# Diagonal tap weights, gate halves and decay products moved in a one-core block kernel

## The reference, cut to what matters

```
proj = h @ w_in[i]
p_r, p_k, p_v, p_c, z_rwkv, z_conv = split(proj)
# rwkv7: k, r times cumulated decays, triangular inverse per chunk of the keys, state recurrence
y_rwkv = rwkv7_time_mix(h, p_r, p_k, p_v, ...)
# convolution
u, gate = split(p_c)
c = u * sigmoid(gate)
c = causal_depthwise_conv(c, dw, 31 taps) + dw_b
y_conv = silu(layer_norm(c)) @ w_conv_out
merged = sigmoid(z_rwkv) * y_rwkv + sigmoid(z_conv) * y_conv
```

## Time and profile before

| what | value |
| --- | --- |
| median of 3 runs (lowest, highest) | 1400.84 us (1398.81, 1406.21) |
| the profiled execution | 1398.78 us, its span 1396.7 us |
| PE busy | 1332.3 us, 95% of the span |
| DVE busy | 1003.6 us, 72% |
| ACT busy | 772.5 us, 55% |
| POOL busy | 105.7 us, 8% |
| mean granted TensorE clock | 0.981 |

### The profile page before, as it was taken

One profiled execution on the slowest core, in us unless ns is written; L12 is line 12 of the kernel. 1 busy time (PEld: TensorE's weight loads), 2 busy tenths in 40 slices (PEclk: granted clock), 3 DMA queues, 4 the chain that ended last, 5 costly groups with the idle time before them and its releaser, 6 DMA issues.

```text
span 1396.7 us, 30214 instructions
## 1 busy us (share of the span) xinstructions
PE 1332.3 (95%) x12462; PEld 1266.0 (91%) x12462; DVE 1003.6 (72%) x1655; ACT 772.5 (55%) x1348; POOL 105.7 (8%) x133
## 2 busy tenths in 40 slices
PE   5999989999999999999997899999999998999998
PEld 5998948989989999989995799999999887999986
DVE  4769897978876664475899867886565655888754
ACT  4596496549455443454668655444455455644453
POOL 2000100000001110000101001111000100022100
PEclk8999999999999999999999899999999999999999
DMA  7642620213545546546662264556565521555462
GB/s 224 186 147 94 211 92 3 93 63 111 191 152 161 185 137 209 187 129 204 195 207 83 75 197 154 185 175 197 174 202 173 163 86 43 200 182 184 155 214 69
DMA packets 199859, 212.71 MB, mean 152 GB/s; under 512 B 8972, under 2 KB 191020, under 8 KB 199612
## 3 DMA queue, kind: packets, MB, share of 16 engines
q1 hardware_dynamic: 197180, 201.46, 45.2%
q0 software_dynamic: 2464, 9.52, 2.3%
q10 hardware_dynamic: 96, 0.02, 0.0%
HBM read 209.33 MB, written 1.65 MB: 151 GB/s over the span
## 4 chain that ended last, share of the span: by engine, by line
PE 83%; DVE 8%; ACT 4%; SPq 2%; issue 1%; DMA 1%; DVEq 0%; ACTq 0%
PE pb L450 21%; PE pb L452 21%; PE pb L451 21%; DVE w_lo L496 1%; PE pb L2678 1%; PE pb L2679 1%; PE pb L2677 1%; PE pb L2198 1%; ACT pj L961 1%; PE pb L2187 1%; SPq L602 1%; DVE pj L1626 1%; PE pb L2604 1%; DMA raw<-in_ffn_w_down_dram 1%; PE pb L2302 1%
## 5 line engine op out<-in xcount | busy, mean ns | idle before, releaser
L490 ACT ACTIVATE w_hi<-raw 128x1024 fp32r<-128x1024 f32 (+2 forms) x384 | 396.7, 1041 | 317.4 <-PE pb L452 248.4
L496 DVE TENSOR_TENSOR w_lo<-raw,w_hi 128x1024 fp32r<-128x1024 f32 (+2 forms) x384 | 467.6, 1221 | 136.9 <-ACT w_hi L490 136.0
L450 PE MATMUL pb<-x_hi,w_hi 128*128 128x256 f32 x1920 | 549.6, 286 | 6.0 <-DVE x_lo L1387 3.8
L451 PE MATMUL pb<-x_lo,w_hi 128*128 128x256 f32 x1920 | 546.5, 285 | 0.0
L452 PE MATMUL pb<-x_hi,w_lo 128*128 128x256 f32 x1920 | 546.4, 285 | 0.0
L450 PEld LDWEIGHTS pb<-x_hi,w_hi 128*128 128x128 f32 x1920 | 371.7, 194 | 9.2 <-DVE w_lo L496 6.6
L451 PEld LDWEIGHTS pb<-x_lo,w_hi 128*128 128x128 f32 x1920 | 371.7, 194 | 0.2
L452 PEld LDWEIGHTS pb<-x_hi,w_lo 128*128 128x128 f32 x1920 | 371.5, 193 | 0.0
L742 POOL TENSOR_TENSOR sub<-sub,rstd 128x256 f32<-128x256 f32 x66 | 71.9, 1104 | 593.0 <-ACT sub L1113 593.0
L450 PE MATMUL pb<-act_hi,w_hi 128*128 128x256 f32 x392 | 112.1, 286 | 3.5 <-DVE w_lo L496 3.5
L452 PE MATMUL pb<-act_hi,w_lo 128*128 128x256 f32 x392 | 111.8, 285 | 0.0
(11 more groups left out here) (344 smaller groups left out, 2197.7 us busy)
## 6 DMA issues: line engine op xcount, KB each, us to landing
raw<-in_ffn_w_up_dram SPq DMA_DIRECT2D x55, 1024.0 KB, 5.1
raw<-in_w_in_dram SPq DMA_DIRECT2D x28, 1024.0 KB, 5.1
raw<-in_ssd_w_in_dram SPq DMA_DIRECT2D x20, 1024.0 KB, 5.4
raw<-in_ffn_w_down_dram SPq DMA_DIRECT2D x16, 1024.0 KB, 5.1
raw<-in_fox_w_in_dram SPq DMA_DIRECT2D x16, 1024.0 KB, 5.8
raw<-in_ffn_w_down_dram SPq DMA_DIRECT2D x16, 896.0 KB, 5.2
raw<-in_ffn_w_gate_dram SPq DMA_DIRECT2D x11, 1024.0 KB, 5.3
raw<-in_ssd_w_out_dram SPq DMA_DIRECT2D x8, 1024.0 KB, 5.2
```

What stands on the lines that cost most here:

```text
L450: pe.matmul(o, w_hi[m][:, k, :], hi[:, k0 + k, :], start=first and k == 0, stop=False)
L451: pe.matmul(o, w_hi[m][:, k, :], lo[:, k0 + k, :], start=False, stop=False)
L490: act.activation(piece(ly, u, w_hi[m], nk, m), raw_piece(ly, u, s, nk, m), ACT.Copy).then_inc(sem("w_hi_ready"), 1)
L496: dve.tensor_tensor(piece(ly, u, w_lo[m], nk, m), raw_piece(ly, u, s, nk, m), piece(ly, u, w_hi[m], nk, m).bitcast(F32), ALU.subtract).the ...
```

## The change

- The ring of diagonal blocks gets 56 places in place of 24: 32 in the slot ZC and 24 in the last six tiles of the slot ZR. ScalarE writes the first 56 blocks (28 taps) inside `ug`, three taps behind each block from block 4, in place of the first 24 behind the sigmoid. At block 4 it first waits for `PAIRS_MADE`, at block 9 for `R_DECAYED`. `DIAG_LEAD` is 22 in place of 8.
- The gate's sigmoid and the product u times gate are made in two halves of four tiles: the first on ScalarE at block 13 and on VectorE at block 14, the second behind `ug`. TensorE waits for the first alone (`GLU_MADE` stays 4; `INVERSES_MADE` becomes 6). ScalarE no longer waits for `GLU_MADE` before its next weights.
- The mixes of v come behind blocks 0 to 3, and the two decay products behind blocks 5 and 6, after the triangular eviction. `lab_t` moves to other tiles of `sub`, since TMP is still read by then.
- The two memsets of `mt` move to GpSimd, between the two hops of its transfers. VectorE waits for them before the first substitution step that reads.
- `SUB_STEPS` holds one step more, so that 15 steps lie in `ug`; the first of the larger corner steps takes the place of the last small one behind `ug`.
- The third `z` eviction, not the ninth, waits for the end of the convolution, as ZR now holds blocks.

The diff, cut to its core:

```diff
-        PE_TILES, NDIAG, DIAG_LEAD = 2 * PE_PAIRS, 24, 8
-        diag = [slot(ZC)[:, i // 4, HEAD * (i % 4):HEAD * (i % 4) + HEAD] for i in range(NDIAG)]
+        PE_TILES, NDIAG, DIAG_LEAD = 2 * PE_PAIRS, 56, 22
+        diag_tiles = [slot(ZC)[:, i, :] for i in range(KC)] + [slot(ZR)[:, i, :] for i in range(2, KC)]
+        diag = [t[:, HEAD * i:HEAD * i + HEAD] for t in diag_tiles for i in range(4)]
+        DIAG_BLOCK, DIAG_STEPS = 4, 3
-        LAB_BLOCK, SUB_BLOCK, SUB_STEPS = 2, 8, (3, 3, 2, 2, 1, 1, 1, 1)
+        LAB_BLOCK, SUB_BLOCK, SUB_STEPS = 2, 8, (3, 3, 3, 2, 1, 1, 1, 1)
-        lab_t = region[:, 0:RWKV_HEADS * T // 4]
+        lab_t = flat_sub[:, 2048:2048 + RWKV_HEADS * T // 4]
...
             pool.wait_ge(sem("mixed"), 3 * KC)
+            link(pool.memset(mt, 0.0))
+            link(pool.memset(mt.rearrange("p s t -> p (s t)")[:, 0:CHUNK * CHUNK:CHUNK + 1], 1.0))
+            pool.nop().then_inc(sem("pool_stages"), 1)
...
+            def gate_half(h):
+                act.wait_ge(sem("evac_done"), L["ug"].evac0 + BANKS + KC + 4 * h + 4)
+                t = slot(GATE)[:, 4 * h:4 * h + 4, :]
+                act.activation(t, t, ACT.Sigmoid).then_inc(sem("gate_ready"), 1)
-            def v_mixes(u, m):
+            def ug_stages(u, m):
+                i = M_PER_UNIT * u + m
                 if u == 0:
                     mix_keep(2, (2 * m, 2 * m + 1))
+                if i == DIAG_BLOCK:
+                    act.wait_ge(sem("dve_stages"), PAIRS_MADE)
+                if i == 9:
+                    act.wait_ge(sem("dve_stages"), R_DECAYED)
+                if i >= DIAG_BLOCK:
+                    step = DIAG_STEPS * (i - DIAG_BLOCK)
+                    tap_weights(0, step, min(step + DIAG_STEPS, NDIAG // 2))
+                if i == M_PER_UNIT * len(L["ug"]) - 3:
+                    gate_half(0)
...
             z_head(LOOKAHEAD)
-            act.wait_ge(sem("evac_done"), L["ug"].evac1 + BANKS)
-            act.activation(slot(GATE), slot(GATE), ACT.Sigmoid).then_inc(sem("gate_ready"), 1)
+            gate_half(1)
...
-            act.wait_ge(sem("dve_stages"), PAIRS_MADE)
-            tap_weights(0, 0, NDIAG // 2)
-            act.wait_ge(sem("dve_stages"), R_DECAYED)
             scale_keys(0)
-            act.wait_ge(sem("dve_stages"), GLU_MADE)
+            v_rows(0)
             for j in range(BANKS, BANKS + Z_EARLY):
                 z_head(j)
-            v_rows(0)
             tap_weights(0, NDIAG // 2, CONV_TAPS)
...
-                if i == 8:
+                if 8 <= i < 12:
+                    mix_shift(2, (2 * (i - 8), 2 * (i - 8) + 1))
+                if i == 13:
                     go(tt(bk_v[:, :, 0, :], chunks(K), chunks(TMP), ALU.mult))
-                if i == 9:
+                if i == 14:
                     go(tt(slot(R), slot(R), slot(W), ALU.mult))
                     sync()
                     dve.nop().then_inc(sem("dve_stages"), 1)
-                if 9 <= i < 13:
-                    mix_shift(2, (2 * (i - 9), 2 * (i - 9) + 1))
...
+            def glu(h):
+                k = slice(4 * h, 4 * h + 4)
+                dve.wait_ge(sem("gate_ready"), h + 1)
+                link(tt(slot(U)[:, k, :], slot(U)[:, k, :], slot(GATE)[:, k, :], ALU.mult))
+                dve.nop().then_inc(sem("dve_stages"), 1)
...
-                if i == SUB_BLOCK - 1:
-                    dve.wait_ge(sem("mixed"), 3 * KC)
-                    link(dve.memset(mt, 0.0))
-                    link(dve.memset(mt.rearrange("p s t -> p (s t)")[:, 0:CHUNK * CHUNK:CHUNK + 1], 1.0))
+                if i == M_PER_UNIT * len(L["ug"]) - 2:
+                    glu(0)
...
             substitute(done, done + 1)
-            dve.wait_ge(sem("gate_ready"), 1)
-            link(tt(slot(U), slot(U), slot(GATE), ALU.mult))
-            dve.nop().then_inc(sem("dve_stages"), 1)
+            glu(1)
```

More of the change, by code:

```diff
@@ L373, in z_bank @@
             return pb[6 - j % 2][:, T:2 * T]
-        BONUS_MADE, PAIRS_MADE, R_DECAYED, GLU_MADE, INVERSES_MADE = 1, 2, 3, 4, 5
-        STATE_ZEROED = 1
+        BONUS_MADE, PAIRS_MADE, R_DECAYED, GLU_MADE, INVERSES_MADE = 1, 2, 3, 4, 6
+        ONES_SET, STATE_ZEROED = 1, 2
         def pe_layer(pe, ly, hi, lo, in_ready, in_base, hook=None, after_two=None, halfway=None, spread=None, before_last=None):
@@ L913, in v_stages, with tap_weights @@
                     act.activation(bonus, pb[4][0:RWKV_HEADS, 0:T], ACT.Copy).then_inc(sem("bonus_ready"), 1)
-            def v_mixes(u, m):
+            def tap_weights(q, first, last):
+                for s in range(first, last):
+                    for c in range(2):
+                        n = 2 * (CONV_TAPS * q + s) + c
+                        if n >= NDIAG and c == 0:
+                            act.wait_ge(sem("tap_summed"), (n - NDIAG) // 2 + 1)
+                        act.activation(diag[n % NDIAG], ident2[:, :], ACT.Copy,
+                                       scale=par_col("conv_dw_pe", 2 * (CONV_TAPS * q + CONV_TAPS - 1 - s) + c)).then_inc(sem("tap_ready"), 1)
+            def gate_half(h):
[4 more added lines that the diff above has]
+                i = M_PER_UNIT * u + m
                 if u == 0:
                     mix_keep(2, (2 * m, 2 * m + 1))
+                if i == DIAG_BLOCK:
[7 more added lines that the diff above has]
+                    gate_half(0)
             act_layer(act, L["rk"], rk_mixes, begin=lambda: norm_root(0), nxt=L["lora_in"])
@@ L920, in _ @@
             act_layer(act, L["v"], v_stages, nxt=L["ug"])
-            act_layer(act, L["ug"], v_mixes, nxt=L["z"])
+            act_layer(act, L["ug"], ug_stages, nxt=L["z"])
             def z_head(j):
@@ L952, in scale_keys @@
                 ins.then_inc(sem("bk_scaled"), 1)
[L954 to L962, removed]
             def conv_pair(q):
@@ L1560, in substitute @@
                     if t == 1:
+                        dve.wait_ge(sem("pool_stages"), ONES_SET)
                         dve.wait_ge(sem("sub_dma"), 80)
@@ L1597, in z_evac @@
                     dve.wait_ge(sem("block_done"), L["z"].item0 + j + 1 + BANKS)
-                    if j == KC:
+                    if j == Z_EARLY:
                         dve.wait_ge(sem("tap_summed"), CONV_TAPS * PE_PAIRS)
```

## The result

| what | before | changed kernel |
| --- | --- | --- |
| median of 6 runs each (lowest, highest) | 1399.26 us (1398.54, 1406.21) | 1392.23 us (1388.62, 1393.38) |
| the profiled execution, its span | 1398.78 us, 1396.7 us | 1393.38 us, 1391.3 us |
| mean granted TensorE clock of it | 0.981 | 0.981 |

The ratio is 0.9931, with a 95% interval from 0.9913 to 0.9949: 7.0 us faster by the medians, 5.4 us by the two profiled executions. The forecast was 1392.6 us and 7.2 us.

A forecast was written before the change was run, and what follows sets the result against it. ScalarE's diagonal blocks were taken to bound the convolution, VectorE's slack to limit the gain: 5.5 + 2.8 - 1.1 = 7.2 us off 1398.78 gave 1391.6, with the median put 1.0 above at 1392.6 us; range 1388.0 to 1398.0.

The forecast's parts named there:

- Blocks inside ug, gate halves at no cost: In ug, six blocks a step (1.45 us) fit ScalarE's 1.76 us idle time; the gate halves cost nothing.
- Start of the convolution: TensorE's wait for u times gate goes, and the convolution starts at 180.0, 3.8 us earlier.
- Speed: In the convolution 62 taps take 25.0 us at 0.404 a tap, ending at 205.0, 9.8 us earlier.
- Rival 2: Convolution taps stay at 0.48 us as TensorE sets that pace; gain 5.0 us, 1394.8 us; chance 0.10.
- Landing of the gathers: GpSimd's gathers start at 144.2, take 10.0 us and land at 154.2, ahead of VectorE's substitution steps.
- s: How much earlier VectorE's events come, set by the gathers' landing: 2.8 us, at most 4.3.
- Rival 1: Gathers land no earlier, s = 0; gain 4.4 us, 1395.4 us; chance 0.16.
- rival 3: GpSimd's memsets and issue are held up and gathers land at 165 to 168: 3 to 6 us slower; chance 0.07.
- The smaller of 9.8 and 5.5 + s: Gain at chunk 0's state products: TensorE's 9.8 us, or VectorE's slack of 5.5 plus s if smaller.
- The loss behind the wait: In chunk 0 TensorE waits 1.5 us for u, and the lower clock behind it costs 1.1 us.
- From chunk 1 on VectorE and TensorE stand to each other as before, so the rest only moves.: In the recurrence from chunk 1 on, the claim that nothing further is gained or lost.
- The point: The forecast median of new runs, 1392.6 us, a gain of 7.2 us; chance 0.56.

The follow-up runs named there:

- e1: Changed kernel with the 24-place ring back, first 24 blocks made behind the sigmoid's second half, none inside ug: 1398.52 us, ratio 0.999 to the kernel before.
- e2: Changed kernel, but TensorE waits for both halves of u times gate: 1398.01 us, ratio 0.9988 to the kernel before.
- e4: Changed kernel with one of VectorE's 12 early taps moved behind chunk 0 (4, 4, 4, 4, 4): 1393.49 us, ratio 0.996 to the kernel before.
- e3: Changed kernel with the decay products and mixes back ahead of the triangular eviction: 1398.64 us, ratio 0.9997 to the kernel before.
- e11: Same edit to the changed kernel as e4, run again on another chip: 1392.85 us, ratio 0.9927 to the kernel before.
- e6: Changed kernel with the two memsets of the block buffer back on VectorE: 1392.64 us, ratio 0.9941 to the kernel before.
- e5: Changed kernel with VectorE's taps as 11 early, then 4, 4, 4, 3, 5: 1389.61 us, ratio 0.9909 to the kernel before.
- e7: Changed kernel with chunk 1's products computed twice and chunk 5's three times: 1389.74 us, ratio 0.9915 to the kernel before.
- e8: Changed kernel with taps 4, 4, 4, 3, 5 and chunk 5's products computed twice: 1388.85 us, ratio 0.9915 to the kernel before.
- e12: Same edit to the changed kernel as e8, run again on another chip: 1388.22 us, ratio 0.9904 to the kernel before.
- e9: The changed kernel again, unedited: 1391.28 us, ratio 0.9929 to the kernel before.
- e10: The changed kernel once more, unedited, on another chip: 1392.56 us, ratio 0.994 to the kernel before.

## Why the prediction was right, and where it was off

- *Blocks inside ug, gate halves at no cost.* Right: TensorE's chunk products start 47.6 us behind the first triangular products, 47.7 before.
- *Start of the convolution* at 180.0: 179.09. Of the 0.9 us between them 0.5 is the earlier start of this execution; the rest is the 0.2 left for block 15 and the cancelling terms, which came out better.
- *Speed.* 25.0 us foretold, 25.4 measured, 0.41 us a tap, and ScalarE done at 199.1 (201 foretold). Rival 2, with 0.48 a tap, is out.
- *Landing of the gathers.* 153.2 in place of 154.2. Two errors in it cancel: the memsets cost the start 1.85 us (2.03 us of wait, then 141.81 to 143.66) where 1.4 were put, and the gathers took 9.6 us where 10.0 were put. Of the 1.0 us left, 0.5 is the earlier start of this execution and the rest an eviction and a write that came a little earlier than put. So s was 3.3 by the last step (200.80 against 204.1), of which 0.5 is that earlier start; 2.8 foretold. Rival 1 and rival 3 are out. For the latter, the issue of the gathers ran beside the first decay product (142.88 to 145.16) in 3.16 us, as before; that a memset would be held by such a product isn't tested here, as the long one ended before it began.
- *The smaller of 9.8 and 5.5 + s.* Right: the copy ended 8.9 us earlier, with 5.5 + 3.3 = 8.8. TensorE waited 1.41 us (1.5 foretold), and the state's products came 8.3 earlier net of the earlier start. `e1` and `e2` show it from TensorE's side, `e4` from VectorE's. What the prediction left out is that a late landing reaches TensorE's own chain in `ug` as well (`e3`).
- *The loss behind the wait.* 1.1 foretold, 1.3 measured in chunk 1.
- *"From chunk 1 on VectorE and TensorE stand to each other as before, so the rest only moves."* This step failed. The wait in chunk 4 is nearly the same (2.64 us against 2.20), yet from chunk 3's y to chunk 5's it takes 30.0 us in place of 26.9. That isn't one bad draw. The three kernels that undo a part, which make chunk 0's y only 1.0 to 3.4 us ahead of the kernel before, counted from the triangular products, have 26.8 to 27.0 there. The changed kernel has 30.0, 30.0 and 28.6 in its three profiles, and the others that come early and keep the wait, `e4`, `e11` and `e6`, 28.7 to 29.5. Those that come early with that wait at 1.0 us or less (`e5`, `e7`, `e8`, `e12`) have 25.7 to 26.8. The wait alone (2.2 us) doesn't bring the long stretch of low clock, nor does the earlier time alone; why both together do stays open. It costs the change some 2 to 3 us.
- *The point.* 1392.6 against 1392.23, and 7.2 us against 7.0 (first six runs), 7.3 (equal clock), 8.5 (medians of 65 and 20 runs) and 5.4 (the profiled pair). That the point is so near is in part luck. Between the two profiled executions 5.4 us were gained and not 7.2, mainly by the loss in chunk 4, so the sum was 1.8 us too hopeful. And the changed kernel's profiled execution stood 1.0 us above the median of its 20 runs, where the forecast had put a median 1.0 above such an execution: 2.0 us too careful. The two cancel. The kernel before's profiled execution stood 2.15 us below the median of its 65 runs; why the medians lie 8.5 us apart where the pair's traces account for 5.4 stays open beyond that draw.

## What to carry to other kernels

When two engines' chains meet, price the shortening of one by the slack of the other, and look for what sets the other: here a landing of four small transfers that an unrelated pair of products held up. A resource that is short in one stretch (places for blocks, ScalarE's time) can be stocked in an earlier stretch in which that engine idles. And at this size look at the granted clock before you explain a profile: `e4`'s profiled execution stood 6.3 us below the median of its own 7 runs.

## What the runs showed of the hardware that was not expected

- The lower clock level stands where TensorE had no wait for it: in `e2` and `e5` the turns of chunk 0 took 1.91 and 1.79 us with no wait recorded in the 13 us ahead of them, and in `e9` and `e10` it also stands in chunk 1, where no wait is recorded either. In the changed kernel's first profile chunk 2's wait of 0.44 us had no lower clock behind it; in the earlier trace rows 0.45 us had. So by these rows a recorded wait right ahead is neither needed for it nor enough. The Trainium skill (TensorE: Matmul & The Clock Gate, Part 1) says that how many matmuls of one kernel run at the lower clock varies from run to run, and these traces agree: the changed kernel's turns of chunk 1 took 1.06 us in one profile and 1.91 and 1.92 in the two others.
- A wait of 2.6 us cost more than itself in chunk 4: the products behind it took 1.97 us in place of 1.15 and the following ones 1.86 in place of 1.07. In `e12`, with other work in that wait, the first took 1.15. But in `e4` they took 1.15 behind a wait of 2.65 us too, and the low clock came later.
- The same four gathers took 9.3 to 10.0 us to land where they started at 143.0 to 143.7 (changed kernel, `e1`, `e2`, `e9`, `e10`), and 10.6 and 10.8 us where they started at 146.5 and 147.3 (before, `e3`).
- Two memsets between a transfer's landing and the next transfers on GpSimd cost 1.85 us for 1.13 us of work (0.96 and 0.17): the rest, 0.7 us, lies in front of the issue.
